# A streaming encoder step on one core: query weights kept through two tiles, queries formed tile by tile, gates and state updates moved behind the streams' chain

## What is computed

```python
h = h * lax.rsqrt(jnp.mean(h * h, axis=-1, keepdims=True) + EPS) * g_hn.astype(f32).reshape(H_M, DH_M)
h = h.reshape(B, L, D_MLSTM) * jax.nn.sigmoid(o.astype(f32))
...
C_new = decay[..., None, None] * C + jnp.einsum('bhs,bshv,bshk->bhvk', wk, v, k)
...
def peer(x, w_pq, subkeys, pu, pv):
    qp = (x @ w_pq).reshape(T, PEER_HEADS, 2, D_PKEY // 2)
    s = jnp.einsum('thcd,hcnd->thcn', qp, subkeys).astype(f32)
    s1, i1 = lax.top_k(s[:, :, 0], PEER_TOPK)
    s2, i2 = lax.top_k(s[:, :, 1], PEER_TOPK)
    cand = (s1[..., :, None] + s2[..., None, :]).reshape(T, PEER_HEADS, PEER_TOPK * PEER_TOPK)
    ...
    u = pu[eidx]
    vv = pv[eidx]
    a = jax.nn.gelu(jnp.einsum('thkd,td->thk', u, x).astype(f32))
    return jnp.einsum('thk,thkd->td', (g * a).astype(vv.dtype), vv).astype(x.dtype)
```

## Time and profile before

| what | value |
| --- | --- |
| median of three runs | 1288.58 us (1286.77 to 1292.61) |
| the profiled execution's own time | 1286.57 us |
| its span, from first to last instruction | 1284.8 us |
| mean granted TensorE clock | 0.969 of full speed |
| TensorE busy | 1123.2 us (87%) |
| VectorE busy | 812.7 us (63%) |
| POOL busy | 711.5 us (55%) |
| ScalarE busy | 458.4 us (36%) |
| bytes by row gathers | 402.68 MB of 459.15 |

### The profile page before, as it was taken

One profiled execution on the slowest core, in us unless ns is written; L12 is line 12 of the kernel. 1 busy time (PEld: TensorE's weight loads), 2 busy tenths in 40 slices (PEclk: granted clock), 3 DMA queues, 4 the chain that ended last, 5 costly groups with the idle time before them and its releaser, 6 DMA issues.

```text
span 1284.8 us, 12644 instructions
## 1 busy us (share of the span) xinstructions
PE 1123.2 (87%) x3320; PEld 550.7 (43%) x3320; DVE 812.7 (63%) x1910; ACT 458.4 (36%) x1354; POOL 711.5 (55%) x898
## 2 busy tenths in 40 slices
PE   6999999999998899999877878878878888888886
PEld 4655656577443455555432333333223222222222
DVE  4356413669997747888977677676555555555554
ACT  2012202222443533444443343343334444434443
POOL 1000000215766656567698666666876878887760
PEclk9999999999999999999988879888998999999999
DMA  9655412148999999999999999999999999999994
GB/s 345 156 150 225 172 66 99 66 180 362 425 424 424 424 426 421 423 403 407 419 420 426 425 426 426 426 425 425 426 425 425 426 425 426 426 427 426 426 426 196
DMA packets 70179, 459.15 MB, mean 357 GB/s; under 512 B 7428, under 2 KB 15976, under 8 KB 18160
## 3 DMA queue, kind: packets, MB, share of 16 engines
q0 software_dynamic: 55296, 402.68, 74.8%
q1 hardware_dynamic: 13984, 55.17, 12.2%
q10 hardware_dynamic: 848, 0.71, 0.2%
HBM read 450.82 MB, written 7.71 MB: 357 GB/s over the span
## 4 chain that ended last, share of the span: by engine, by line
DMA 40%; PE 39%; POOL 8%; DVE 6%; issue 4%; ACT 2%; ACTq 0%; POOLq 0%; DVEq 0%; SPq 0%
DMA arena<-in_peer_uv,arena 38%; PE ps L1254 13%; PE ps L940 9%; PE ps L946 5%; POOL arena L672 4%; PE ps L1160 3%; PE ps L1240 3%; DVE arena L1717 3%; POOL arena L671 2%; POOL arena L665 1%; ACT arena L863 1%; DMA out_new_C_p<-arena 1%; DMA arena<-in_w_pq 1%; PE ps L1218 1%; PE ps L1132 1%
## 5 line engine op out<-in xcount | busy, mean ns | idle before, releaser
L1254 PE MATMUL ps<-arena 128*128 128x512 f32 x1536 | 742.7, 625 | 140.2 <-ACT arena L863 136.9
L1717 DVE CUSTOM_DVE_ANT_0 arena<-arena 128x1024 f32<-128x1024 f32 x384 | 467.5, 1231 | 300.2 <-DMA arena<-in_peer_uv,arena 297.8
L1254 PEld LDWEIGHTS ps<-arena 128*128 128x128 f32 x1536 | 287.5, 197 | 568.4 <-issue 287.7
L672 POOL DMA_INDIRECT arena<-in_peer_uv,arena x256 | 306.4, 1197 | 53.7 <-issue 46.5
L855 ACT ACTIVATE arena<-arena 128x1 f32<-128x1 f32 x384 | 77.7, 202 | 485.8 <-DVE arena L1717 484.8
L646 POOL DMA_INDIRECT arena<-in_peer_uv,arena x128 | 150.7, 1177 | 25.3 <-issue 15.1
L863 ACT ACTIVATE arena<-arena 128x128 f32<-128x128 f32 x384 | 154.2, 402 | 18.8
L857 ACT ACTIVATE arena<-arena 128x1 f32<-128x1 f32 (+1 forms) x384 | 113.1, 294 | 27.9 <-ACT arena L855 1.9
L671 POOL TENSOR_TENSOR arena<-arena 128x1 f32<-128x1 f32 x256 | 111.2, 435 | 14.6 <-POOL arena L665 8.1
L940 PE MATMUL ps<-arena 128*128 128x384 f32 (+1 forms) x336 | 111.1, 487 | 0.0
L645 POOL TENSOR_TENSOR arena<-arena 128x1 f32<-128x1 f32 x128 | 55.1, 431 | 86.3 <-PE ps L1254 84.6
(11 more groups left out here) (234 smaller groups left out, 740.1 us busy)
## 6 DMA issues: line engine op xcount, KB each, us to landing
arena<-in_w_in SPq DMA_DIRECT2D x8, 2048.0 KB, 10.7
arena<-in_w_pq SPq DMA_DIRECT2D x6, 2048.0 KB, 9.3
arena<-in_peer_uv,arena POOLq DMA_INDIRECT x384, 27.3
arena<-in_w_out SPq DMA_DIRECT2D x4, 1024.0 KB, 6.0
arena<-in_state_C SPq DMA_DIRECT2D x1, 2064.0 KB, 7.5
out_new_C_s<-arena SPq DMA_DIRECT2D x1, 2064.0 KB, 6.6
arena<-in_cache_k SPq DMA_DIRECT2D x4, 512.0 KB, 11.1
arena<-in_cache_v SPq DMA_DIRECT2D x1, 2048.0 KB, 10.7
```

Of the source, the lines that this page charges most:

```text
L672: nc.gpsimd.indirect_dma_start(slots[HALF * g + s], None, d["peer_uv"], bass.IndirectOffsetOnAxis(ap=isl[g][:, s:s + 1], axis=0)).then_inc ...
L1254: last = mm(ps[:, BANKS + half, :], diag[:, s, :], slots[SLOTS * h + s][:, DM + 512 * half:DM + 512 * half + 512], start=first and s == 0, ...
L1717: v.tensor_tensor_reduce(slots[k][:, 0:DM], slots[k][:, 0:DM], hn[t], 1.0, 0.0, ALU.mult, ALU.add, aslot[:, s:s + 1]).then_inc(a_ok, 1)
```

## The change

- The query weights get places of their own: chunks 0 and 1 (`W2`, `PQ1`) are loaded before the gathers begin and stay through the first two tiles; chunks 2 and 3 go to `W0` and `W1` once the halves of the output weights there have been used. Nothing is read twice. Those four places become slots 8 to 15 for the last tile alone; the first two tiles have 8 slots each.
- The queries are formed one tile at a time, in parts of 128 columns (`qs`): those of tile 2 and of tile 0 in the first tile, those of tile 1 in the second. The streams' first chunk is split in two (`qh`, one head each), so that the first head can be matched and routed after half of it.
- The gates are a sigmoid on ScalarE. `mo0` and `mo1` move behind the streams' first scores; the product for the prompt tiles is a step of piece 0, and `hmT0` and `hmT1` a step of piece 1.
- `CN1`, `CN2` and `CN3` move to later places, and POOL's weights for them have two buffers.
- The first gather waits for CN3 alone; the other seven first ones also wait until the new state has been written out (`state_out`), two of them for `hmT1`.
- The routing is in steps of one head throughout; the last tile's stands in the second tile by piece.

The diff, cut to its core:

```diff
+    first = [[] for _ in range(PIECES)]
+    second = [[] for _ in range(PIECES)]
+
+    def parts(steps, q, every, *what):
+        for part in range(4):
+            steps[q + every * part] += [(*what, part)]
+
+    first[1] += [("hmT", a), ("hmT", b)]
+    parts(first, 1, 1, "qs", 2, 1)
+    first[5] += [("sc", 2, 1)]
+    parts(first, 6, 1, "y", a, 0)
+    parts(first, 10, 1, "y", b, 0)
+    parts(first, 14, 1, "y", a, 1)
+    parts(first, 18, 1, "qs", 2, 2)
+    first[22] += [("sc", 2, 2)]
+    parts(first, 24, 1, "y", b, 1)
+    parts(first, 32, 1, "qs", 2, 3)
+    first[37] += [("sc", 2, 3)]
+    first[38] += [("hnT", a, 0), ("hnT", a, 1)]
+    for c, q in enumerate((39, 43, 47, 51)):
+        parts(first, q, 1, "qs", a, c)
+        first[q + 4] += [("sc", a, c)]
+    second[0] += [("hnT", b, 0), ("hnT", b, 1)]
+    for c, q in enumerate((1, 9, 17, 25)):
+        parts(second, q, 2, "qs", b, c)
+        second[q + 8] += [("sc", b, c)]
...
+    put(0, ("gated",))
+    put(1, ("subkeys", 2, 0, (1,)), *pairs(2, 1), *experts(1))
+    put(6, *sub(2, 1), *pairs(2, 2, 3), *experts(2))
+    put(12, ("y", a, 0))
+    put(15, ("y", b, 0))
+    put(18, ("y", a, 1))
+    put(23, *sub(2, 2), *pairs(2, 4, 5), *experts(3))
+    put(29, ("y", b, 1), ("square", a), ("square", b), ("scale", a), ("scale", b))
+    put(38, *sub(2, 3), *pairs(2, 6, 7), *experts(4))
+    for t, part in ((a, 5), (b, 9)):
+        for c in range(4):
+            q = (44, 50, 56, 62)[c] if t == a else PIECES + (10, 18, 26, 34)[c]
+            put(q, *sub(t, c), *pairs(t, 2 * c, 2 * c + 1), *experts(part + c))
...
-        slot_at = [AT["W2"], AT["W2"] + 2 * DM, AT["W3"], AT["W3"] + 2 * DM] + [AT[f"SL{k}"] for k in range(4, 8)]
-        slot_after = ["qs0"] * 2 + ["qs1"] * 2 + ["hmT1"] * 4
-
-
-        slot_at += [AT[f"X{k}"] for k in range(8)]
+        slot_at = [AT[f"SL{k}"] for k in range(SLOTS)]
+        slot_after = ["CN32"] + ["mo1"] * 5 + ["hmT1"] * 2
+
+        slot_at += [AT[k] + half for k in ("W2", "PQ1", "W0", "W1") for half in (0, 2 * DM)]
...
-        stream_chunk = ["W2", "W3", "PQA", "PQB"]
-        prompt_chunk = [("PQA", "again0"), ("W0", "again1"), ("PQA", "pq2"), ("PQB", "pq3")]
+        query_chunk = ["W2", "PQ1", "W0", "W1"]
...
             filled(sp, "mv2")
-            for i in range(2):
-                load_w(whigh[:, i], d["w_out"][i][:, 4:8], "high")
-            filled(sp, "NUM1")
+            load_w(wbuf["W0"], d["w_out"][0], "out0")
+            filled(sp, "mq3")
             sp.dma_start(subk, d["subkeys"]).then_inc(subk_in, 16)
-            filled(sp, "mq3")
-            for i in range(2):
-                load_w(wlow[:, i], d["w_out"][i][:, 0:4], "low")
+            load_w(wbuf["W1"], d["w_out"][1], "out1")
+            load_w(wbuf["PQ1"], d["w_pq"][1], "pq1")
             filled(sp, "mk3")
             load_w(wbuf["W2"], d["w_pq"][0], "pq0")
-            filled(sp, "mo1")
-            load_w(wbuf["W3"], d["w_pq"][1], "pq1")
-
-            filled(sp, "CN32")
-            load_w(wbuf["PQA"], d["w_pq"][2], "pq2")
             sp.wait_ge(cn_ok, HM)
             sp.dma_start(d["new_C_s"], CT).then_inc(state_out, 16)
             sp.dma_start(d["new_C_p"], CP).then_inc(state_out, 16)
-            sp.wait_ge(state_out, 32)
-            load_w(wbuf["PQB"], d["w_pq"][3], "pq3")
-            filled(sp, "qs3")
+            filled(sp, f"y{ORDER[2]}0")
+            load_w(wbuf["W0"], d["w_pq"][2], "pq2")
+            filled(sp, f"y{ORDER[2]}1")
+            load_w(wbuf["W1"], d["w_pq"][3], "pq3")
...
                         if first and not odd:
                             filled(pool, slot_after[HALF * g + s])
+                            if HALF * g + s:
+                                pool.wait_ge(state_out, 32)
...
-                read(f"mo{t}", mo[:, t, :], ACT.Exp, bank(f"mo{t}"), scale=-1.0)
+                read(f"mo{t}", mo[t], ACT.Sigmoid, bank(f"mo{t}"))
...
             head_keys(3)
-            new_state(1)
-            pe.wait_ge(w_in["high"], 32)
+            pe.wait_ge(w_in["out0"], 16)
+            pe.wait_ge(w_in["out1"], 16)
             was_read(pe, "oS1")
             for i in range(2):
                 project_out("ya", 2, i)
             head_sum(3)
-            project("mo", 0)
+            new_state(1)
             turn_heads(2)
-            new_state(2)
-            pe.wait_ge(w_in["low"], 32)
             was_read(pe, "hmT2")
             for i in range(2):
                 project_out("y", 2, i)
-            project("mo", 1)
+            new_state(2)
...
             pe.wait_ge(hn_ok, 1)
             for i in range(2):
                 turn_hn(2, i)
+            was_read(pe, "hnT21")
+            head_queries(0)
+            head_match(0)
             new_state(3)
-            was_read(pe, "hnT21")
-            stream_queries(0)
-            turn_heads(0)
-            turn_heads(1)
-            pe.wait_ge(subk_in, 16)
-            scores(2, 0)
-            stream_queries(1)
-            scores(2, 1)
-            stream_queries(2)
-            stream_queries(3)
-            for q in range(PIECES):
-                for what, *k in query_steps()[q]:
-                    if what == "qq":
-                        prompt_query(*k)
-                    elif what == "y":
-                        if k == [ORDER[1], 0, 0]:
-                            was_read(pe, "hmT1")
-                            was_read(pe, "op11")
-                        project_out("y", *k)
-                    elif what == "hnT":
-                        pe.wait_ge(hn_ok, NT)
-                        turn_hn(*k)
-                        if k == [ORDER[2], 1]:
-                            was_read(pe, f"hnT{ORDER[2]}1")
-                    else:
-                        scores(*k)
-                i, s = divmod(q * PIECE, SLOTS)
-                weigh(0, i, i == 0, i == ROUNDS - 1, 0, range(s, s + PIECE))
+            project("mo", 0)
+            project("mo", 1)
+            head_queries(1)
+            head_match(1)
...
-            new_state(1)
-            output_gates(2, 1)
+            dve.wait_ge(ghn_in, 16)
+            was_read(dve, "mo2")
+            v.tensor_tensor(mo[2], mo[2], ghn, ALU.mult)
             for i in range(2):
                 add_mix("ya", 2, i)
             head_out(HM - 1)
             gated(2, 1)
-            new_state(2)
+            v.tensor_tensor(hflat[:, 0:2, :], hflat[:, 0:2, :], over(ghn, 1, 2), ALU.mult)
+            new_state(1)
             for i in range(2):
                 add_mix("y", 2, i)
             dve.wait_ge(gffn_in, 16)
             square_h(2, (2,))
             scale_h(2, (2,))
-            output_gates(0, 2)
-            gated(0, 2)
-            new_state(3)
+            new_state(2)
...
+            route_subkeys(2, 0, (0,))
+            route_pairs(2, 0, 1)
+            route_experts(0, 0)
+            route_experts(0, 1)
+            new_state(3)
```

More of the change, by code:

```diff
@@ L48 @@
 WROUNDS = HK // WIDE
-LATE = 12
 PIECE = 2
@@ L118, in psum_plan @@
     add("A", "mo2")
[L119 to L130 removed]
+    add("V", "ST3", "mkt3", "ya20", "ya21", "NUM3", *heads("CN", 3, 1))
+    add("A", "hmT2")
+    add("V", "y20", "y21", *heads("CN", 3, 2))
+    add("A", "hnT20", "hnT21", "qh0")
+    add("V", "sh0", *heads("CN", 3, 3))
+    add("A", "mo0", "mo1", "qh1")
+    add("V", "sh1")
+    for what, *k in sum(query_steps()[0] + query_steps()[1], []):
+        if what in ("sc", "hnT", "hmT") or k[-1] == 0:
             add("V" if what in ("sc", "y") else "A", psum_name(what, k))
@@ L656, in gather_wide @@
                     back = WIDE
-                    if first and n == 1:
+                    if first:
                         back = SLOTS if g < 2 else 0
```

353 lines of the change are left out of this document (162 added, 191 removed).

## The result

The changed kernel takes 1302.8 us (median of four runs, 1302.6 to 1308.2), the kernel before 1288.0 beside it: a ratio of 1.0122, 95% interval 1.0100 to 1.0145. It is slower by some 15 us, where 1283 was forecast and the range ended at 1297. The profiled execution took 1302.64, with a span of 1300.8: 16.0 us more than before.

What follows compares the result with a forecast made beforehand. It took the kernel to be bound by its stream of 384 row gathers, 2.464 us each. Start -9.0, first tile +1.0 and second +3.4 made -4.6 us, so 1283 us was forecast, range 1271 to 1297.

Steps and rivals of the forecast that it cites:

- The start: Work ahead of the first gathers: gather 1 issued 5.1 us earlier, landing 9.0 earlier (bounds 5 and 11.5).
- Gating was to end at 251.9: VectorE at the start: gating of the normalised head ends 4.70 us behind NUM3, which ends at 247.2.
- the gap: Start, the 4.70 us between NUM3 and gating's end: CN1 stands in it and costs nothing.
- The projection: Start, output projection matmuls mo2 on TensorE: taken to last 7.03 us, like mo0.
- first MAX8: Start, VectorE's first routing step: comes at 271.5 us, not 285.45, with first expert numbers 13.9 earlier.
- 8.9 us: Start, write of the new state: lasts 8.9 us from 283.2, freeing every slot but the first at 292.1.
- rival B: Start: the state's write decides; some 3 us are left and the tiles take them back, 1288 us; chance 0.12.
- The first tile: Counted from gather 1's landing: 1 us more than the 7.4 lost now, bounds 7 less and 5 more.
- A hole of about 1 us: First tile's beginning: two slots wait for hmT1, behind the weighing of gathers 0 and 1, about 1 us.
- The second tile: With 8 slots, own queries and routing: 323.6 us against 320.2, 3.4 more; bounds -3.6 and +8.8.
- C: Second tile: TensorE at half clock, paid for with 8 slots; +16 on the sum, 1298 us; chance 0.13.
- The third tile: Last tile: keeps its 16 slots, so nothing changes; its last dot 317 us behind the second's.

Runs made afterwards that it cites:

- a7: Changed kernel with all slots at multiples of 512 bytes, then slots 0, 2 and 5 moved on by 128 bytes: 1296.3 us (1.0071).
- a8: a7 with GpSimd's last weights after gating, state written in two pieces, prompt gating and head turning earlier, only slots 5 to 7 behind the write: 1285.0 us (0.9978).
- a11: a8 with the slots above word 27,760 moved to multiples of 256 bytes of the partition: 1281.2 us (0.9946).
- b5: Kernel before with everything from word 35,056 of the arena on, slots 4 to 7 included, moved up by 448 bytes: 1283.1 us (0.9966).
- b1: Kernel before with slot 15 alone, used only in the second and third tile, starting 48 bytes later: 1287.4 us (0.9999).

## Why the prediction was wrong

By the terms of its sum, start, first, second and third tile, it forecast -9.0, +1.0, +3.4 and nothing; measured were +3.1, +7.2, +3.1 and +2.6, together 16.0.

**The start: the step that failed.** The forecast put gather 1 at 292.6 and its landing at 297.5; it was issued at 304.12 and landed at 309.6, 12.1 late and 3.1 later than before. By its own steps:
- NUM3 ended some 0.8 late (CN1 behind it started at 247.97). Gating was to end at 251.9 with VectorE's old durations; it ended at 255.78, and 3.1 of that is GpSimd beside it. The trace of before had GpSimd's work elsewhere, and the step asked only what VectorE and TensorE do. CN1, which was costed at nothing in the gap, is what let GpSimd start there: its end (250.3) releases the last head's weights, since these have two buffers now.
- The projection was to take 7.03. The gap had been seen (4.70) and its effect on the clock not: 10.00, 3.0 late, and then the queries 5.47 for 3.66. So the first MAX8 came at 280.4 for 271.5 (the terms named for it add up to 271.2), still 5 us ahead of before.
- "8.9 us" for the write of the state became 11.2, beside gather 0. The bound of the whole step, 5 to 11.5 earlier, left this out.

That the write decides (rival B) was the right mechanism, but B put its end at 293.7 and the time at 1288: "the tiles take them back". It ended at 303.3, and they did not.

**The first tile.** Forecast +1.0, bounds -7 and +5; counted from gather 1's landing it was +7.2. "A hole of about 1 us" for the two slots behind hmT1 is where it was mis-sized: GpSimd stood 5.8 us, and the DMA fell to 390 and 344 GB/s. From gather 1's dot to the tile's last, a7 takes 333.5 and a8, in which the waits are short, 331.1: the waits cost some 2.4. The level cost some 1.7, an estimate (below). The kernel before takes 328.7 by the same count, with no more of its eight slots at a multiple than a8, so some 3 us of the tile's loss, of which 1 was forecast, stay open.

**The second tile.** Forecast +3.4, measured +3.1; that the two are so near is at least in part luck, for the lower level, which the forecast left out, is in the measured one. In a7, where 3 of 8 slots are at a multiple of 256 as 6 of 16 were before, the tile takes 320.5, 0.3 over the kernel before. So there the break cost hardly more than before, and in the changed kernel the lower level would make up the sum. But in the best layouts, all slots at 309 ns, it is 320.7 (a11) against 317.5 (b5): 3.2 again, as forecast. How much eight slots cost at the break stays open. C did not come: the granted clock fell only behind the break (0.60 and 0.71 in the ten us from 655), and from 700 to 800 us the granted clock was 1.00, where it had been 0.86. Whether the short routing steps did that, or the queries that TensorE now forms there (91.8 of the 100 us busy, 82.3 before), was not tried.

**The third tile.** "Keeps its 16 slots: nothing" was wrong by 2.6. The term that was missing is the new table of addresses: it was read for what shares memory with what, not as something with a speed. By the table it costs 2.6 where none of the slots in use is at a multiple and 6 of 16 were, as in the third tile, and by estimate in the second; the first went from 2 of 8 to none, an estimate of 1.7 by the same slope. That is 7 in all, and a7 gave back 6.5.

**The account.** The 15 us are some 6.5 to 7 of level and the 8.5 that a7 still takes over the kernel before; by its rows some 7 of these lie in the start and the first tile. With the state's write, the turned heads and GpSimd out of the way they become a gain of 2.9 (a8).

## What to carry to other kernels

When work is moved into a gap, ask what it releases on the engines that were not looked at: here a product moved forward let GpSimd start beside the critical VectorE chain. When a gather moves forward, list what each buffer waits for; the last wait, not the route to the indices, sets the stream. And treat a new memory layout as an edit with a price: look at where the buffers of a saturated stream start, modulo 256 bytes of the partition, with the place of the arena itself counted in.

## What was not expected of the hardware

- A gather's 8 KB packets take 309 ns or about 313 (packet records), by where the slots start: ten of sixteen at a multiple of 256 bytes of the partition give 427 GB/s, six 426, three 424, none 422, and each slot at a multiple keeps one behind it at 309 as well. One more start off the boundary, at 48 bytes (b1), changed nothing, since it was off before.
- VectorE's 384- and 512-wide products took 2.07 and 2.28 us beside GpSimd instead of 0.56 and 0.69, each time ending 0.4 to 0.6 us behind GpSimd's instruction (253.05 and 255.23), about its usual length.
- A gather with little else on the DMA queues landed in 5.5 us (the prediction took 4.9, and had 4.4 as a second estimate); the 2.38 MB write of the state took 11.2 us beside one gather, 8.9 before.
